# Sample attention inside an expert loop, cut into pieces of one product per loop slot

## What is computed

```
kp = ck[page_table].reshape(DB, -1, H, HD)
vp = cv[page_table].reshape(DB, -1, H, HD)
lfp = clf[page_table].reshape(DB, -1, H)
c_all = cumsum(concatenate([lfp, logf], axis=1), axis=1).transpose(0, 2, 1)
bias = c_all[:, :, P:, None] - c_all[:, :, None, :]
s = concatenate([einsum('bqhd,bkhd->bhqk', q, kp), einsum('bqhd,bkhd->bhqk', q, k)], -1) * scale + bias
p = softmax(where(mask, s, MASK_VALUE))
o = einsum('bhqk,bkhd->bqhd', p[..., :P], vp) + einsum('bhqk,bkhd->bqhd', p[..., P:], v)
```

## Time and profile before

| | |
|---|---|
| median of three runs | 4754.21 us (4746.54 to 4771.33) |
| profiled execution | 4763.2 us, of which the span is 4761.4 us |
| mean granted TensorE clock | 0.827 |
| busy share of the span: TensorE, VectorE, ScalarE, POOL | 78%, 56%, 48%, 29% |
| chain that ended last: DMA, TensorE, VectorE, ScalarE | 31%, 25%, 11%, 7% |

### The profile page before, as it was taken

One profiled execution on the slowest core, in us unless ns is written; L12 is line 12 of the kernel. 1 busy time (PEld: TensorE's weight loads), 2 busy tenths in 40 slices (PEclk: granted clock), 3 DMA queues, 4 the chain that ended last, 5 costly groups with the idle time before them and its releaser, 6 DMA issues.

```text
span 4761.4 us, 53894 instructions
## 1 busy us (share of the span) xinstructions
PE 3708.2 (78%) x19049; PEld 2813.8 (59%) x19049; DVE 2660.2 (56%) x5621; ACT 2261.7 (48%) x4152; POOL 1400.3 (29%) x1160
## 2 busy tenths in 40 slices
PE   7998799999958888768667778788767666766666
PEld 5666577755735555655455656556655555555555
DVE  3666233344157975564455437966653586756754
ACT  3222111111115565566443445566575566666665
POOL 0000000000003333333443323433333355655644
PEclk9999899999979999888665569999878766666666
DMA  2000100032339999999987889999999999999998
GB/s 76 27 27 27 51 23 23 10 102 95 120 110 415 419 398 414 381 392 404 371 319 251 306 305 382 408 417 414 371 414 376 388 405 421 421 419 420 416 413 341
DMA packets 278736, 1367.53 MB, mean 287 GB/s; under 512 B 33671, under 2 KB 89415, under 8 KB 138213
## 3 DMA queue, kind: packets, MB, share of 16 engines
q0 software_dynamic: 158720, 1143.02, 58.9%
q1 hardware_dynamic: 119789, 221.64, 13.3%
HBM read 1335.23 MB, written 29.69 MB: 287 GB/s over the span
## 4 chain that ended last, share of the span: by engine, by line
DMA 31%; PE 25%; DVE 11%; ACT 7%; issue 3%; POOL 1%; SPq 1%; another core or an unknown queue 0%; DVEq 0%; ACTq 0%; POOLq 0%
DMA p_ring<-in_peer_uv,p_idx 25%; PE psum L1709 8%; DVE p_ring L1777 6%; PE psum L1085 4%; DMA t_w<-in_w_query 4%; PE psum L1164 4%; ACT p_ring L1743 3%; PE psum L1582 2%; PE psum L1089 2%; DMA group<-in_x_all 2%; PE psum L1130 1%; DVE group L1314 1%; ACT p_act_w L1740 1%; POOL p_ring L1689 1%; PE psum L1092 1%
## 5 line engine op out<-in xcount | busy, mean ns | idle before, releaser
L1709 PE MATMUL psum<-ident,p_ring 128*128 128x128 f32 x8704 | 1528.6, 334 | 829.5 <-ACT p_ring L1743 812.0
L1689 POOL DMA_INDIRECT p_ring<-in_peer_uv,p_idx x1088 | 1324.4, 1217 | 2309.9 <-PE psum L1709 1802.6
L1709 PEld LDWEIGHTS psum<-ident,p_ring 128*128 128x128 f32 x8704 | 1262.2, 174 | 1183.1 <-ACT p_ring L1743 1073.9
L1777 DVE CUSTOM_DVE_ANT_0 p_ring<-p_ring,p_xn 128x1024 f32<-128x1024 f32 x1088 | 1329.1, 1223 | 967.2 <-DMA p_ring<-in_peer_uv,p_idx 956.2
L1743 ACT ACTIVATE p_ring<-p_ring,p_act_w 128x1024 f32<-128x1024 f32 x1088 | 1249.6, 1149 | 35.5
L1738 ACT ACTIVATE p_gl<-p_hid 128x1 f32<-128x1 f32 x1088 | 218.8, 201 | 1181.1 <-DVE p_hid L1777 1168.4
L1085 PE MATMUL psum<-group,t_w 128*128 128x384 f32 (+1 forms) x1344 | 452.5, 477 | 8.1 <-DMA t_w<-in_w_conv 8.1
L1164 PE MATMUL psum<-group,t_w 128*128 128x384 f32 (+1 forms) x768 | 280.5, 501 | 87.9 <-DMA t_w<-in_w_query 86.7
L1740 ACT ACTIVATE p_act_w<-p_gl,p_w 128x1 f32<-128x1 f32 x1088 | 320.5, 295 | 35.3
L1085 PEld LDWEIGHTS psum<-group,t_w 128*128 128x128 f32 x1344 | 247.7, 195 | 131.0 <-DMA t_w<-in_w_conv 8.3
L1674 POOL MEMSET c_mean_w<- 128x128 f32 x1 | 0.2, 204 | 946.8 <-POOLq L86 946.8
(11 more groups left out here) (289 smaller groups left out, 3786.2 us busy)
## 6 DMA issues: line engine op xcount, KB each, us to landing
t_w<-in_w_merge SPq DMA_DIRECT2D x72, 768.0 KB
t_w<-in_w_query SPq DMA_DIRECT2D x48, 576.0 KB
p_ring<-in_peer_uv,p_idx POOLq DMA_INDIRECT x1088
group<-in_cache_kT SPq DMA_DIRECT2D x64, 256.0 KB
group<-in_cache_v SPq DMA_DIRECT2D x64, 256.0 KB
t_w<-in_w_conv SPq DMA_DIRECT2D x24, 512.0 KB
t_w<-in_w_outs SPq DMA_DIRECT2D x24, 512.0 KB
h_w<-in_w_hgrn SPq DMA_DIRECT2D x16, 512.0 KB
```

What stands on the lines that cost most here:

```text
L1689: pool.indirect_dma_start(ring[:, at % RING, :], None, io["peer_uv"], bass.IndirectOffsetOnAxis(ap=idx[:, u, c:c + 1], axis=0)).then_inc(r ...
L1709: last = pe.matmul(acc[u][:, k * P:(k + 1) * P], ring[:, at % RING, D + k * P:D + (k + 1) * P], ident[:, :], start=(c == 0 and k % 4 == 0) ...
L1777: dve.tensor_tensor_reduce(out=ring[:, g, 0:D], in0=ring[:, g, 0:D], in1=xn[:, u, :], scale=1.0, scalar=0.0, op0=ALU.mult, op1=ALU.add, ac ...
```

## The change

The pieces of the sample attention are laid over the slots anew. The score products of parts 0 and 1 stand one per slot: bias in slot 0, four products in slots 1 to 4, bias in 5, four products in 6 to 9, part 2 in slot 10. The value products get a generator of their own (`sample_values`), in half products (pages 0 to 3; pages 4 to 7 and the new keys), one half per slot from slot 15 to 22, that is slots 2 to 9 of the following batch. The maximum and the exp are due in slot 11, the transposes in 12 and 13, the copies of the result in slot 23 (slot 10 of the next batch), and `prepare` three slots later than it was. K pages count on two semaphores, one for each four pages; pages and forget factors are due two per slot and one per slot. The second trunk plan starts at slot 428 for 417, and the choice for tile 6 eleven slots later with the same end. Products, their operands and their number stay the same.

```diff
--- before.py
+++ after.py
@@ -823,9 +823,9 @@
 
...
 START = -600
-PLANS = (Plan(0, START, 10, 8, 20, 5, 4), Plan(1, 0, 7, 5, 22, 5, 4), Plan(2, 417, 6, 5, 20, 5, 4))
+PLANS = (Plan(0, START, 10, 8, 20, 5, 4), Plan(1, 0, 7, 5, 22, 5, 4), Plan(2, 428, 6, 5, 20, 5, 4))
 SAMPLE, BATCH = 308, 13
-CHOOSE = {3: 37, 6: 65}
+CHOOSE = {3: 37, 6: 76}
 
...
 def tiles():
@@ -902,7 +902,7 @@
         w_loaded = [m.sem(f"t_w_loaded{u}") for u in range(3)]
...
         xnb_loaded = [m.sem(f"p_xnb_loaded{u}") for u in range(2)]
-        k_loaded, v_loaded = m.sem("g_k_loaded"), m.sem("g_v_loaded")
+        k_loaded, v_loaded = [m.sem(f"g_k{u}_loaded") for u in range(2)], m.sem("g_v_loaded")
         lf_loaded = [m.sem(f"g_lf_loaded{n}") for n in range(PAGES)]
...
         s_stored = [m.sem(f"t_s_stored{u}") for u in range(2)]
@@ -1496,7 +1496,7 @@
 
...
             for b in range(DB):
-                yield SAMPLE + BATCH * b - 7
+                yield SAMPLE + BATCH * b - 4
                 if b == 0:
...
                         sp.wait_ge(xn_stored[j], after(16 * 2))
@@ -1504,14 +1504,16 @@
                 else:
...
                 for n in range(PAGES):
+                    yield SAMPLE + BATCH * b - 4 + n // 2
                     page = sp.value_load(pages[0:1, b * PAGES + n:b * PAGES + n + 1], min_val=0, max_val=PHYS - 1)
-                    sp.dma_start(kc[:, n, :], io["cache_kT"][rows(page), :]).then_inc(k_loaded, 16)
-                yield SAMPLE + BATCH * b + 4
+                    sp.dma_start(kc[:, n, :], io["cache_kT"][rows(page), :]).then_inc(k_loaded[n // 4], 16)
+                yield SAMPLE + BATCH * b + 10
                 if b == 0:
...
                 for n in range(PAGES):
+                    yield SAMPLE + BATCH * b + 10 + n // 2
                     page = sp.value_load(pages[0:1, b * PAGES + n:b * PAGES + n + 1], min_val=0, max_val=PHYS - 1)
...
 
@@ -1526,6 +1528,7 @@
                 else:
...
                 for n in range(PAGES):
+                    yield SAMPLE + BATCH * b - 12 + n
                     pool.indirect_dma_start(lfc[:, n * PAGE:(n + 1) * PAGE], None, io["cache_lfT"],
...
                                             ).then_inc(lf_loaded[n], 16)
@@ -1540,26 +1543,24 @@
                 pe.wait_ge(bq_ok, after(b + 1))
...
                 pe.wait_ge(exp_ok, after(b))
-                for n in range(PAGES):
-                    pe.wait_ge(k_loaded, 16 * PAGES * (b + 1))
                 for part, (off, n) in enumerate(CHUNKS):
                     out = sps[:, off:off + n]
-                    if part:
-                        yield at + 3 * part
+                    yield at + 5 * part
                     if part == 2:
...
                     for x in range(4):
-                        if part < 2 and x % 2 == 1:
-                            yield at + 3 * part + (x + 1) // 2
+                        if part < 2:
+                            yield at + 5 * part + 1 + x
+                            pe.wait_ge(k_loaded[part], 16 * 4 * (b + 1))
                         keys = kc[:, 4 * part:4 * part + 4, x * P:(x + 1) * P] if part < 2 else k_new[:, x, :]
...
                 for half in range(2):
-                    yield at + 10 + 2 * half
+                    yield at + 12 + half
                     pe.wait_ge(diag_ok, after(b + 1))
...
                     for n in range(4 * half, 4 * half + 4):
@@ -1568,15 +1569,19 @@
                         pe.wait_ge(tn_ok, after(b))
...
                     last.then_inc((ta_ps, tb_ps)[half], 1)
-                yield at + 15
+
+        def sample_values(pe):
+            for b in range(DB):
+                at = SAMPLE + BATCH * b + 15
+                yield at
                 pe.wait_ge(tb_ok, after(b + 1))
...
                 for x in range(4):
-                    if x:
-                        yield at + 15 + x
                     for n in range(9):
+                        if n in (0, 4):
+                            yield at + 2 * x + n // 4
                         width = P if n < 8 else NS
...
                         last = pe.matmul(po[:, x * 32:x * 32 + 16], vals, pT[0:width, n, x * 32:x * 32 + 16], start=(n == 0), stop=(n == 8))
@@ -1585,13 +1590,13 @@
         def sample_act(act):
...
                 at = SAMPLE + BATCH * b
-                yield at + 8
+                yield at + 11
                 act.wait_ge(max_ok, after(b + 1))
...
                 for half in range(2):
-                    yield at + 11 + 2 * half
+                    yield at + 13 + half
                     act.wait_ge((ta_ps, tb_ps)[half], after(b + 1))
...
                     act.activation(pT[:, 4 * half:4 * half + 4, :], pb[3].rearrange("p (n r) -> p n r", n=4), ACT.Copy).then_inc((ta_ok, tb_ok)[half], 1)
@@ -1602,17 +1607,17 @@
                 at = SAMPLE + BATCH * b
...
                     yield from prepare(dve, 0)
-                yield at + 7
+                yield at + 11
                 dve.wait_ge(sc_ps, after(b + 1))
                 dve.tensor_reduce(nmax[:, :], sps, AX.X, ALU.max, negate=True).then_inc(max_ok, 1)
-                yield at + 9
+                yield at + 12
                 dve.wait_ge(exp_ok, after(b + 1))
...
                     yield from prepare(dve, b + 1)
-                yield at + 19
+                yield at + 23
                 dve.wait_ge(pv, after(b + 1))
...
                     for hh in range(2):
@@ -1621,7 +1626,7 @@
 
...
             at = SAMPLE + BATCH * b
-            yield at - 5
+            yield at - 2
             if b == 0:
...
                 for u in range(2):
@@ -1632,14 +1637,14 @@
             dve.tensor_tensor_scan(c_all[:, 0:W], ones[:, 0:1].broadcast_to([64, W]), lfc, 0.0, ALU.mult, ALU.add).then_inc(c_ok, 1)
...
             dve.tensor_scalar(c_all[:, W:W + NS], c_new[:, :], c_all[:, W - 1:W], None, ALU.add).then_inc(cn_ok, 1)
-            yield at - 4
+            yield at - 1
             dve.wait_ge(cn_ok, after(b + 1))
...
             dve.tensor_tensor(bias_q, bias_q, sel[:, 0, :], ALU.add).then_inc(bk_ok, 1)
-            yield at - 3
+            yield at
             dve.wait_ge(bk_ok, after(b + 1))
...
             dve.tensor_copy(q_rows[0:64, :, 0:DT], q_new[0:64, :, b * DT:(b + 1) * DT])
@@ -1696,7 +1701,7 @@
             for at in range(START, 0):
...
                     x.to(at)
-            trunk = [Pace(units_pe(pe, PLANS[1])), Pace(rest_pe(pe, PLANS[1])), Pace(sample_pe(pe)), Pace(units_pe(pe, PLANS[2])),
+            trunk = [Pace(units_pe(pe, PLANS[1])), Pace(rest_pe(pe, PLANS[1])), Pace(sample_pe(pe)), Pace(sample_values(pe)), Pace(units_pe(pe, PLANS[2])),
                      Pace(rest_pe(pe, PLANS[2]))]
...
             for t, u, n, slots in tiles():
```

## The result

The changed kernel takes 4681.66 us (median of four runs, 4676.78 to 4686.50) against 4752.71 us of the kernel before: ratio 0.9844, 95% interval [0.9815, 0.9873]. It is 71 us (1.6%) faster, and the interval lies clear of 1; the forecast was 4785 us and slower. Its profiled execution took 4680.1 us (span 4678.1 us), that of before 4763.2 us.

What follows compares the result with a forecast made beforehand. DMA bounds the tail; in the sample stage TensorE at half clock, then chain waits. 30 + 7 x 68 + 50 = 556 against 531.4 us, with plan 2 and choice 4, 31 more: 4785 us, 0.65% slower (chance 0.45), range 4772 to 4812.

Steps and rivals of the forecast that it cites:

- the clock in slots 2 to 9: Slots mixing ring, score and half value products: clock 0.50, one slot of eight at full clock, 44.5 us a batch.
- the full clock holds: Rival: TensorE stays at 1.00 through slots 2 to 9, period 48 us, 4636 us; chance 0.15 including a good part.
- part-way cases: Some of slots 2 to 9 at full clock; five of eight give period 57.2 us and 4709 us.
- the half per cent: 24 us, about what a measurement can tell from no change; said to be passed with five slots at full clock.
- Eight single slots: Score products one per slot instead of two bursts: 11.4 us of TensorE more a batch at the lower clock.
- The chain: Slots 10 to 14 (maximum, exp, scan, transposes): 25.2 us, with a third of the way towards full clock.
- its two bounds: Slots 10 to 14 take 26.6 us at TensorE's lower clock and 22.2 at the full one.
- Pages: K and V page transfers on SP stay in blocks of eight; two K semaphores gain 0, TensorE's page waits cost nothing.
- The ends: Sample stage outside the seven periods: 30 us to the first maximum, 50 us behind the last.
- Plan and choice: Second trunk plan eleven slots later costs 2 us (0 to 3); tile 6's shortened choice costs 4 (0 to 18.7).

Runs made afterwards that it cites:

- e16_after: The changed kernel itself measured again, unaltered, beside two others on one chip: 4686.73 us, ratio 0.9843 to the kernel before.
- e2_fewer: The changed kernel without six of a batch's eight cached-key score products: 4712.19 us, ratio 0.9910 to the kernel before.
- e3_bursts: The changed kernel with the four score products of a part in one slot (1 and 6) instead of four: 4707.15 us, ratio 0.9891 to the kernel before.
- e12_burstfill: e3_bursts plus one never-read product of 512 columns in each of slots 2 to 9: 4702.27 us, ratio 0.9883 to the kernel before.
- e15_valgen: The kernel before with only a separate generator for whole value products, beside the next batch's scores in slots 2 to 5: 4762.54 us, ratio 1.0007.
- e6_chainfill: The changed kernel with never-read products of 512 columns in slots 10, 11, 12 and 15 of the first batches: ratio 0.9854 to the kernel before.
- e4_plan: The kernel before with only the second trunk plan at slot 428 and tile 6's choice eleven slots later: 4772.31 us, ratio 1.0031.
- e18_lflate: The changed kernel with the forget factors' gathers four slots later, GpSimd's wait for the scan left in place: 4662.23 us, ratio 0.9820 to the kernel before.
- e20_lfwait: The changed kernel with the forget factors' gathers and GpSimd's wait for the scan both four slots later: 4660.80 us, ratio 0.9802 to the kernel before.

## Why the prediction was wrong

**The step that failed** is the clock in slots 2 to 9: "it is nearest to the value slots, so 0.50", with one slot of eight at the full clock, 44.5 us. Measured: 29.0 at 0.89 (27.3 at 0.96 in e16_after). These 15 us a batch, over seven batches, are nearly all of the miss: the stage was to take 556 us and took 438.8, and 7 x (68 - 52.6) = 108 of these 117 are the period. I took the mixture's clock from the row that had most of its loads. e2_fewer and e3_bursts show that in these slots, with half a value product each, one narrow product per slot makes the difference (0.89 for 0.63 and 0.57), and e12_burstfill that a throwaway one does it too (0.85).

The rival "the full clock holds", to which the prediction gave 0.15 with its part-way cases, was right in its mechanism. Its size lies between the two times worked out there, 4636 with the clock at 1.00 throughout and 4709 with five of eight slots. (By the prediction's own sum four slots, not five, already pass the half per cent.) The Trainium skill (TensorE: Matmul & The Clock Gate, Why this matters for your kernels) says to keep TensorE busy without gaps for the full clock. That doesn't tell these cases apart: e15_valgen is busy 28.60 of 28.60 us at 0.59 and the value slots of before 22.47 of 22.8 at 0.50, while the changed kernel's 20.83 of 22.00 run at 1.00.

**Eight single slots cost 11.4 us a batch more.** True at the lower clock only; at the full clock a product is 1.05, and TensorE's busy time fell by 6.4 us a batch instead of rising by 11.4.

**The chain.** 25.2 us forecast for slots 10 to 14, 24.7 measured: right. But its two bounds, 26.6 and 22.2 by the clock, were not: e6_chainfill has 0.93 there and no less time. (By halving the rows that the prediction adds up there, the second comes to some 21.5, not 22.2.) TensorE waits for VectorE and ScalarE there, whatever its clock. The saving of some 9 us against the nine slots of before was in the sum; e3_bursts shows it apart, at the low clock, and a loss like e4_plan's 15 us is inside its 0.9891.

**Pages.** SP's blocks of eight stayed, as said. TensorE's wait for K pages, left at nothing, was 4.0 us in all. POOL was costed at nothing; a wait of 77.2 us came. What it costs isn't shown; later gathers (e18_lflate, e20_lfwait) are 11 to 20 us faster by the ratios.

**The ends.** 30 us forecast and 29.3 measured ahead of the first maximum (2393.6 - 2364.3); 50 forecast and 41.3 measured behind the start of the last (2803.1 - 2761.8), at the DMA's pace (share 1.01 in the second window above) and not at the lower clock's.

**Plan and choice.** 2 + 4 forecast, 15 measured by e4_plan; inside the bounds that I gave together (0 to 3, and 0 to 18.7), but split otherwise: by the traces some 7 us each, so the plan was beyond its bound.

Together: the new slots with bursts are worth 65 us (50 in e3_bursts, and the 15 that it pays for plan and choice, if e4_plan's loss is the same there; slots 422 to 767 take 1043.2 us in it, 1040.9 in the changed kernel and 1026.7 in the one before), single products 22 to 25 more, and 15 are given back: 72 to 75, for 71 measured.

## What to carry to other kernels

Work that the bounding engine does slowly is best spread under slots that run anyway; slots beneath a chain of waits are nearly free up to the number that the chain covers (six here) and cost their full price beyond. Before costing a mixture at either clock, find what changes the clock in the trace: here slots bound by weight loads, without one free microsecond, ran at half clock, and one narrow product of 512 columns in each of the new half slots brought the full one in most of them. Where such an assumption carries half of the sum, the forecast's range has to hold both levels.

## What was not expected of the hardware

Added TensorE work made the engine faster: four throwaway products of 32 output rows in each of three value slots raised the clock there from 0.52 to 0.66 in the mean and from 0.50 to 0.81 in one batch, and one of 512 columns in each of eight slots from 0.57 to 0.85 in the mean and to 1.00 in one batch. And leaving out six of eight products made the same slots longer, 30.6 us for 29.0 in the mean. At the full clock the added products cost about what they brought.
